# Expert blocks of a token-routed layer: the second product one block later, the middle product in one sum of 512 columns

## The chip, the cores and the metric

The kernel runs on one core of a Trainium2 chip, in one launch. The metric is device time in microseconds (us) from the start of the program to its end.

## What is computed

One layer of a diffusion backbone over 1024 tokens (and 256 context tokens), width 1024. A mixer comes first and is not touched. Then each token goes to two of 16 experts, and the sums are added to the residual stream:

```python
def _moe(xf, w_router, router_bias, w1, w3, w2):
    ...
    padded = (counts + MOE_BLOCK - 1) // MOE_BLOCK * MOE_BLOCK
    ...
    def expert_block(args):
        xblk, e = args
        return (jax.nn.silu(xblk @ w1[e]) * (xblk @ w3[e])) @ w2[e]
```

The 2048 rows (1024 tokens, two experts each) are sorted by expert and cut into blocks of 128 rows (MOE_BLOCK), each of one expert. w1 and w3 are 1024 x 512, w2 is 512 x 1024, all float32. How many blocks an expert has depends on the data; with the inputs timed here there are 23 blocks.

## The kernel before, in words

The program is written engine by engine; every order and every wait is spelled out by hand. The mixer and the router take the first 560 us or so. Then VectorE makes the tables: `slot_tok` (which token is in which slot), `tabs` (a word for each block b: its expert, plus 16 if block b+1 has another expert) and the number of blocks `nb`. Each engine then runs a loop over the blocks, unrolled by two, with branches on `nb` and on the word.

**One product as three.** Every float32 operand is split into a high part, rounded to the fp32r type, and the low rest. `product` (L1536) issues three matmuls for one: high x high, high x low, low x high. For weights, ScalarE copies half a matrix from `raw` to `w1h`, `w3h` or `w2h` (`high`, L729) and VectorE subtracts to make `w1l`, `w3l`, `w2l` (`low`, L1183). For a block's tokens they make `xTh`, `xTl` (`turn_out`), for the hidden rows `hTh` and `hTl` (`hidden_high`, `hidden_low`). There is one set of split weights: the halves of the next expert's w1 can be written only when the last matmul of this expert has read the old half.

**One block on TensorE**, in order (from L1543): 24 matmuls of 512 columns for x @ w1 (bank 2); then x @ w3 in two sums of 256 columns each, q = 0 into bank 3 and q = 1 into bank 4, 24 matmuls each, so that the first half of the hidden rows can be multiplied, transposed and split while the second half is summed; two transposes of the first hidden half stand within the second sum (L1570); then `turn_block(b + 1)`, the eight transposes of the next block's tokens (L1534); then 24 matmuls of 512 columns for hidden @ w2, with the other two transposes (L1590) after the first six.

**The weights' way in.** `raw` has 4 places of one matrix (2 MB) each. SyncE's `load_expert` (L390) issues the 48 loads in the order w1, w3, w2 of expert 0, 1, 2 and so on, each into the place after the one before. A load waits until the matrix that lay in its place, four loads back, is split: w1 of expert e waits for the split of w2 of e-2, w3 of e for w1 of e-1, w2 of e for w3 of e-1.

```python
                    elif not (first and n == 3):
                        sp.wait_ge(w_split[(j + 2) % 3], 2 * e - (2 if j == 0 else 0))
```

In the last block of expert e the two engines split all three matrices of e+1: w1 behind the two halves of x @ w1, w3 behind each sum of 256 columns, w2 behind the two halves of hidden @ w2 (L766 to L790, L1220 to L1235). GpSimd gathers the rows of block b+1 (`gather`, an indirect DMA from `hx_rows` to `xg`), and adds the finished rows into `x_rows` (`add_rows`, L529, an indirect DMA that adds). After the last one comes a short final part that reads `x_rows`, normalises and stores.

Of the kernel before, what the change touches and what calls it, by code (L numbers as in the profile page):

```python
# [26 lines left out]
ALU = mybir.AluOpType  # L27
# [45 lines left out]
def hybrid_block(nc, x, c, ctx_in, c_ctx, w_mod, b_mod, norm1, norm2, w_in, w_gk2, b_gk, w_pool,  # L73
                 pool_scale, gla_gain, w_out, w_router, router_bias, w1, w3, w2, norm_f, inv_counts, out):
    with ExitStack() as stack:
# [68 lines left out]
        with nc.sbuf_tensor("lead_columns", [P, O_G + D], F32), \  # L144
# [73 lines left out]
            tok_ready tok_seen dst_ready dst_seen high_seen split_seen load_seen gathered x_turned xh_ready xT_ready l1a_half l1a l1b l1c silu_done hid_a hid_b hta htb  # L218
            hTh_a hTh_b hT_a hT_b
# [104 lines left out]
        for n, shape in dict(sbias=[NX, NE], hi=[32, 2], lo=[32, 2], t1=[32, 1], t2=[32, 1],  # L324
# [4 lines left out]
                             blkf=[2, NX], posf=[2, NX], prior=[NX, 2 * NGR]).items():  # L329
# [3 lines left out]
        assert rt_at <= ARENA  # L333
        cmp16 = at(O_G + HALF, "p (e k) -> p e k", NE * KC, e=NE)
# [14 lines left out]
        ebf = sb("ebf", [P, NB])  # L349
        new_e = sb("new_e", [P, NB - 1])  # L350

        tabs = sb("tabs", [P, NB + 1], I32)
        T_NB = NB
        NEW = NE

        def entry(eng, b):

            word = eng.value_load(tabs[0:1, bass.ds(b, 1)], min_val=0, max_val=NE + NEW - 1)
            return word & (NE - 1), word

        def place_of(e, j):

            return (e * 3 + j + 3) & (PLACES - 1)

# [4 lines left out]
        def _(sp):  # L369
# [19 lines left out]
            def load_expert(e, turn, first=False):  # L389

                for j, w in enumerate((w1, w3, w2)):
# [3 lines left out]
                    elif first and n == 2:  # L395
                        sp.wait_ge(S["pads_stored"], 16 * 2)
# [31 lines left out]
        def _(pool):  # L428
# [66 lines left out]
            for i in range(2, 9):  # L495
                late_bias(i)
            bc = ("box_chain", [NT])
# [17 lines left out]
            pool.wait_ge(S["pads_stored"], 16 * 2)  # L515
# [8 lines left out]
            def add_rows(b, s):  # L524
# [5 lines left out]
                                        in_=ysb[:, s, :], in_offset=None, compute_op=ALU.add).then_inc(S["y_added"], 16)  # L530
# [4 lines left out]
            nb = pool.value_load(tabs[0:1, T_NB:T_NB + 1], min_val=1, max_val=MAXB)  # L535
            pool.wait_ge(S["x_turned"], 1)
            gather(1)
            pool.wait_ge(S["x2_stored"], 16 * NX)
            pool.sem_inc(S["y_free"], 2)
            pool.wait_ge(S["x_turned"], 2)  # L540
            gather(2)
            pool.wait_ge(S["y_ready"], 4)
            add_rows(0, 0)
            with pool.Fori(0, NB // 2) as pair:
                i = pair * 2
                for s in range(2):
                    with pool.If(i + (s + 1) < nb):
                        b = i + (s + 1)
                        with pool.If(b + 1 < nb):
                            pool.wait_ge(S["x_turned"], b + 2)  # L550
                            gather(b + 2)
                        pool.wait_ge(S["y_ready"], 2 * i + (2 * s + 6))
                        pool.sem_inc(S["dst_seen"], 1)
                        pool.wait_ge(S["y_added"], 16 * b)
                        pool.sem_inc(S["y_free"], 1)
                        add_rows(b, 1 - s)
            pool.wait_ge(S["y_added"], 16 * nb)
            pool.sem_inc(S["moe_done"], 1)
# [9 lines left out]
        def _(act):  # L568
# [121 lines left out]
            for t in range(NX + 2):  # L690
# [20 lines left out]
                if 1 <= t <= NX:  # L711
# [7 lines left out]
                    if w == 0:  # L719
                        for spare in (x_dram, hx_dram):  # L720
                            act.dma_start(spare[PADS:PADS + P, :], x2[:, w, :]).then_inc(S["pads_stored"], 16)
# [7 lines left out]
            def high(j, base, k):  # L729
                act.activation(half_of(j, w_hi[j][:, :], k), half_of(j, raw[:, bass.ds(base, UNIT)], k), ACT.Copy).then_inc(w_high[j], 1)  # L730
# [17 lines left out]
            def hidden_high(b, k):  # L748
                act.wait_ge(S["htb" if k else "hta"], b + 1)
                act.activation(hTh[:, k * 256:(k + 1) * 256], ps[:, 5, k * 256:(k + 1) * 256], ACT.Copy)\  # L750
                    .then_inc(S["hTh_b" if k else "hTh_a"], 1)

            def arrived(j, e):
                act.wait_ge(w_loaded[j], 16 * e + 32)
                act.sem_inc(S["load_seen"], 1)

            act.preload_act_table(ACT.Silu)
            turn_out(0)
            with act.Fori(0, NB // 2) as pair:
                i = pair * 2  # L760
                for s in range(2):
                    with act.If(i + s < nb):
                        b = i + s
                        e, word = entry(act, b)
                        with act.If(word > NE - 1):
                            place = [place_of(e, j) for j in range(3)]  # L766
                            arrived(0, e)
                            act.wait_ge(S["l1a_half"], b + 1)
                            act.sem_inc(S["load_seen"], 1)
                            high(0, place[0] * UNIT, 0)  # L770
                            gate_up(b)
                            high(0, place[0] * UNIT, 1)
                            arrived(1, e)
                            act.wait_ge(S["l1b"], b + 1)
                            act.sem_inc(S["load_seen"], 1)
                            high(1, place[1] * UNIT, 0)
                            hidden_high(b, 0)
                            act.wait_ge(S["l1c"], b + 1)
                            act.sem_inc(S["load_seen"], 1)
                            high(1, place[1] * UNIT, 1)  # L780
                            turn_out(b + 1)
                            hidden_high(b, 1)
                            arrived(2, e)
                            act.wait_ge(S["l2_half"], b + 1)
                            act.sem_inc(S["load_seen"], 1)
                            high(2, place[2] * UNIT, 0)
                            act.wait_ge(S["l2_done"], b + 1)
                            act.sem_inc(S["load_seen"], 1)
                            high(2, place[2] * UNIT, 1)
                        with act.Else():  # L790
                            gate_up(b)
                            hidden_high(b, 0)
                            act.wait_ge(S["l1c"], b + 1)
                            turn_out(b + 1)
                            hidden_high(b, 1)
# [11 lines left out]
        def _(dve):  # L807
# [257 lines left out]
            dve.memset(R["cb"][:, :, 0:8], 0.0)  # L1065
            v(dve.memset(R["cb2"][:, :, 0:8], 0.0))
# [56 lines left out]
            def tables():  # L1123
# [4 lines left out]
                v(dve.tensor_reduce(ebf[:, :], cmpb, AX.X, ALU.add))  # L1128
                v(dve.tensor_scalar(ebf[:, :], ebf[:, :], float(NE - 1), None, ALU.min))
# [487 lines left out]
```

## Time and profile before

| | us |
|---|---|
| median of 3 runs | 1023.66 (1022.66 to 1024.78) |
| the profiled execution, its own time | 1024.93 |
| its span in the trace | 1023.1 |
| expert blocks in it, first matmul to last weighing | 566.89 to 989.30, 422.4 |

The span is the time between the first and the last instruction in the trace; 1.8 us of the execution lie around it. TensorE's rows carry modelled ends, so the length of one matmul is more than it costs in a row of them: the distance from one start to the next is what counts. In the windows view, a line has the stretch, its length, each engine's busy time with its count of instructions, TensorE's granted clock as a share of 2.4 GHz, the DMA engines' busy share, and GB/s.

### The profile page before, as it was taken

The numbers are of one execution on the slowest core, as the hardware profiler recorded it, in microseconds if no ns is written. First come the engines' busy times: TensorE is split into PE (matmuls) and PEld (weight loads), VectorE is DVE, ScalarE is ACT, GpSimd is POOL, SyncE is SP. The second block draws the span as 40 slices with busy tenths as digits, with TensorE's granted clock in tenths as the row PEclk, the third lists the DMA queues.
The fourth block names the chain that finished last, engine by engine and source line by source line (L and its number), as shares of the span: only waits on it lengthen the run. The fifth ranks groups of instructions, "written<-read, shape, count | busy, mean of one in ns | idle before, by whom it ended". The sixth has DMA issues, their size and how long they took to land. (4 is left out here: it accounts for less than half of the span.)

```text
span 1023.1 us, 13258 instructions
## 1 busy us (share of the span) xinstructions
PE 938.6 (92%) x4591; PEld 642.6 (63%) x4592; DVE 598.8 (59%) x804; ACT 355.2 (35%) x476; POOL 190.5 (19%) x212
## 2 busy tenths in 40 slices
PE   4899999999999999999955899999999999999960
PEld 1554544445444445656534788898888988888850
DVE  0246666889433335444438575949967456599933
ACT  1333423100011221212123154637745335477613
POOL 5101000000000010011000132323432233243322
PEclk9699999999999999999975899999999999999985
DMA  9923442420200522111183766979998686699928
GB/s 330 395 82 102 147 165 95 152 82 1 83 0 1 211 116 105 42 42 62 62 300 111 288 206 183 334 241 320 380 362 273 184 305 221 185 339 371 320 40 349
DMA packets 76506, 194.11 MB, mean 190 GB/s; under 512 B 3493, under 2 KB 3626, under 8 KB 76474
## 3 DMA queue, kind: packets, MB, share of 16 engines
q1 hardware_dynamic: 64192, 152.05, 40.9%
q0 software_dynamic: 7680, 25.35, 10.2%
q10 hardware_dynamic: 4602, 16.30, 4.0%
q8 instruction: 19, 0.31, 0.1%
q14 instruction: 13, 0.11, 0.0%
HBM read 167.98 MB, written 25.71 MB: 189 GB/s over the span
## 5 line engine op out<-in xcount | busy, mean ns | idle before, releaser
L1325 PE MATMUL ps<-arena 128*128 128x512 f32 x288 | 128.8, 601 | 0.0
L1333 PE MATMUL ps<-arena 128*128 128x512 f32 (+1 forms) x288 | 119.1, 571 | 0.0
L1464 PE MATMUL ps<-arena 128*128 128x512 f32 x256 | 113.3, 595 | 0.0
L1540 PE MATMUL ps<-w3h,xTh 128*128 128x256 f32 x368 | 105.9, 288 | 0.0
L1540 PE MATMUL ps<-w3h,xTl 128*128 128x256 f32 x368 | 104.1, 283 | 0.0
L1540 PE MATMUL ps<-w3l,xTh 128*128 128x256 f32 x368 | 104.1, 283 | 0.0
L1333 PEld LDWEIGHTS ps<-arena 128*128 128x128 f32 x288 | 54.0, 190 | 64.3 <-issue 62.7
L1325 PEld LDWEIGHTS ps<-arena 128*128 128x128 f32 x288 | 54.2, 193 | 62.5 <-issue 62.5
L1187 DVE TENSOR_TENSOR w1l<-raw,w1h 128x2048 fp32r<-128x2048 f32 x30 | 68.6, 2287 | 29.8 <-ACT w1h L730 29.7
L1464 PEld LDWEIGHTS ps<-arena 128*128 128x128 f32 x256 | 47.4, 190 | 54.4 <-issue 53.6
L730 ACT ACTIVATE w1h<-raw 128x2048 fp32r (+1 forms) x32 | 61.1, 1912 | 58.0 <-PE ps L1540 46.2
L1540 PE MATMUL ps<-w2h,hTh 128*128 128x512 f32 x184 | 76.9, 418 | 0.8 <-DVE hTl L1200 0.4
L1540 PE MATMUL ps<-w1h,xTh 128*128 128x512 f32 x184 | 72.7, 395 | 3.2 <-DVE xTl L1180 3.2
L1540 PE MATMUL ps<-w1h,xTl 128*128 128x512 f32 x184 | 72.3, 393 | 0.0
L1540 PE MATMUL ps<-w1l,xTh 128*128 128x512 f32 x184 | 72.3, 393 | 0.0
L1540 PE MATMUL ps<-w2h,hTl 128*128 128x512 f32 x184 | 72.2, 393 | 0.0
L1540 PE MATMUL ps<-w2l,hTh 128*128 128x512 f32 x184 | 72.2, 393 | 0.0
L1187 DVE TENSOR_TENSOR w2l<-raw,w2h 128x2048 fp32r<-128x2048 f32 x32 | 71.8, 2285 | 0.0
L1540 PEld LDWEIGHTS ps<-w3l,xTh 128*128 128x128 f32 x368 | 70.5, 192 | 0.9
L730 ACT ACTIVATE w2h<-raw 128x2048 fp32r (+1 forms) x32 | 61.1, 1917 | 28.9 <-PE ps L1540 22.9
L1540 PEld LDWEIGHTS ps<-w3h,xTh 128*128 128x128 f32 x368 | 70.4, 191 | 0.9
L1187 DVE TENSOR_TENSOR w3l<-raw,w3h 128x2048 fp32r<-128x2048 f32 x31 | 70.9, 2286 | 0.0
(244 smaller groups left out, 1496.5 us busy)
## 6 DMA issues: line engine op xcount, KB each, us to landing
raw<-in_w_dram SPq DMA_DIRECT2D x48, 2048.0 KB, 12.9
arena<-in_w_mod_dram SPq DMA_DIRECT2D x12, 2048.0 KB, 8.0
arena<-in_w_in_dram SPq DMA_DIRECT2D x4, 2048.0 KB, 15.2
x_rows<-arena ACTq DMA_DIRECT2D x9, 512.0 KB, 2.6
hx_rows<-arena ACTq DMA_DIRECT2D x9, 512.0 KB, 2.6
arena<-in_x_dram SPq DMA_DIRECT2D x8, 512.0 KB, 14.5
arena<-in_w_out_dram SPq DMA_DIRECT2D x2, 2048.0 KB, 9.3
arena<-in_x_dram ACTq DMA_DIRECT2D x8, 512.0 KB, 10.5
```

The costliest lines, as they stand in the source:

```text
L730: act.activation(half_of(j, w_hi[j][:, :], k), half_of(j, raw[:, bass.ds(base, UNIT)], k), ACT.Copy).then_inc(w_high[j], 1)
L1187: dve.tensor_tensor(half_of(j, w_lo[j][:, :], k), half_of(j, raw[:, bass.ds(base, UNIT)], k), half_of(j, w_hi[j][:, :], k).bitcast(F32), A ...
L1325: ins = pe.matmul(ps[:, bank, :], hxT[:, k, g[1] * P:(g[1] + 1) * P], w[:, k, :], start=(k == 0), stop=(k == KC - 1))
L1333: ins = pe.matmul(ps[:, bank, 0:m * P], w[:, k, col:col + P], hxT[:, k, t0 * P:(t0 + m) * P], start=(k == 0), stop=(k == KC - 1))
L1464: ins = pe.matmul(ps[:, 5 + h, :], m, w[:, k, :], start=(k == 0), stop=(k == KC - 1))
L1540: ins = pe.matmul(out_ap, parts[l][:, lhs], w_parts[w][:, cols], start=start and n == 0, stop=stop and n == 2)
```

## The change

Four things change, all in the expert blocks.

1. **The second layer comes one block later.** TensorE's body for block b (`pe_block`) is x @ w1 of block b (`gate_part`), four transposes of the hidden rows of block b-1 (`turn_hidden`), x @ w3 of block b (`up_part`), the eight transposes of the tokens of block b+1, and then hidden @ w2 of block b-1 (`out_of_hidden`). Block 0 has a first part of its own in front of the loop, and the last block's hidden @ w2 follows the loop.
2. **x @ w3 is one sum of 512 columns** in bank 3; `hidden`, `hidden_high` and `hidden_low` each work on 512 columns at once, after all of it.
3. **w2 is split at that point.** w2 of expert e was split in the last block of e-1; it is now split in the first block of e (`own_down`), behind the two halves of hidden @ w2 of the block before. The word in `tabs` gets 32 more if block b-1 had another expert. w1 and w3 of the next expert are still split in the last block of this one (`next_gate`, `next_up`).
4. Around it: gathers run one block further ahead; the last block's rows go out from `xg`; the spare rows of `hx_rows` are filled by GpSimd from `ident`, not by ScalarE's queue; the table needs one more small VectorE instruction. `load_expert` is untouched but for the count of `pads_stored`.

```diff
-        def half_of(j, unit, k):
-
-            if j == 1:
-                return unit.rearrange("p (k n) -> p k n", k=KC)[:, :, k * 256:(k + 1) * 256]
+        def half_of(unit, k):
...
@@ ScalarE
+            def next_gate(b, e, k):
+
+                if k == 0:
+                    after(w_loaded[0], 16 * e + 32)
+                after(S["l1a" if k else "l1a_half"], b + 1)
+                high(0, place_of(e, 0) * UNIT, k)
...
+            def own_down(b, e, k):
+
+                if k == 0:
+                    after(w_loaded[2], 16 * e + 16)
+                after(S["l2_done" if k else "l2_half"], b)
+                high(2, place_of(e - 1, 2) * UNIT, k)
...
+            def act_block(b, par):
+                e, word = entry(act, b)
+                with act.If((word & LAST) > 0):
+                    next_gate(b, e, 0)
+                    act.wait_ge(S["hid_done"], b)
+                    gate_up(b)
+                    hidden_high(b - 1)
+                    next_gate(b, e, 1)
+                    next_up(b, e, 0)
+                    turn_out(b + 1)
+                    next_up(b, e, 1)
...
+                with act.If(word > FIRST - 1):
+                    own_down(b, e, 0)
+                    own_down(b, e, 1)
@@ VectorE
+            def dve_block(b, par):
+                e, word = entry(dve, b)
+                with dve.If((word & LAST) > 0):
+                    low(0, place_of(e, 0) * UNIT, e + 1, 0)
+                    hidden_low(b - 1)
+                    low(0, place_of(e, 0) * UNIT, e + 1, 1)
+                    hidden(b)
+                    low(1, place_of(e, 1) * UNIT, e + 1, 0)
+                    turn_out(b + 1)
+                    low(1, place_of(e, 1) * UNIT, e + 1, 1)
...
+                weigh(b - 1, ysb[:, 1 - par, :])
+                with dve.If(word > FIRST - 1):
+                    low(2, place_of(e - 1, 2) * UNIT, e, 0)
+                    low(2, place_of(e - 1, 2) * UNIT, e, 1)
...
+            hidden_low(nb - 1)
+            weigh(nb - 1, xg)
@@ TensorE
-                        for q, done in enumerate(("l1b", "l1c")):
...
-                                ins = product(ps[:, 3 + q, 0:256], x_parts, slice(k * P, (k + 1) * P), (w3h, w3l),
-                                              slice(col, col + 256), k == 0, k == KC - 1)
...
+            turn_x(0)
+            gate_part(0, 0)
+            up_part(0)
+            turn_x(1)
+
+            def pe_block(b, par):
+                e, word = entry(pe, b)
+                pe.wait_ge(S["silu_done"], b)
+                gate_part(b, e)
+                turn_hidden(b - 1)
+                up_part(e)
+                turn_x(b + 1)
+                pe.wait_ge(S["y_ready"], 2 * b)
+                out_of_hidden(b - 1, (e + (word >> 5) * (NE - 1)) & (NE - 1))
+
+            blocks(pe, nb, pe_block)
+            turn_hidden(nb - 1)
+            pe.wait_ge(S["y_ready"], 2 * nb)
+            out_of_hidden(nb - 1, NE - 1)
```

ScalarE's instructions in the last block of an expert, from the first half of w1, before (ISA and REGISTER_ALU are waits and addresses; `arena` at L746 is the silu, at L754 in the changed kernel):

```order
L730 ACTIVATE w1h<-raw 128x2048
L746 ACTIVATE arena<-ps 128x512 [waits l1a]
L730 ISA
L730 ACTIVATE w1h<-raw 128x2048
L730 REGISTER_ALU [waits w_loaded_w3,l1b]
L730 REGISTER_ALU
L730 ISA
L730 ACTIVATE w3h<-raw 128x8x256
L750 ACTIVATE hTh<-ps 128x256 [waits hta]
L730 ISA [waits l1c]
L730 ACTIVATE w3h<-raw 128x8x256
```

and in the changed kernel:

```order
L738 ACTIVATE w1h<-raw 128x2048
L754 ACTIVATE arena<-ps 128x512 [waits l1a,hid_done]
L758 ACTIVATE hTh<-ps 128x512 [waits ht_done]
L738 ISA [waits l1a]
L738 ACTIVATE w1h<-raw 128x2048
L738 REGISTER_ALU [waits w_loaded_w3,l1b_half]
L738 REGISTER_ALU
L738 ISA
L738 ACTIVATE w3h<-raw 128x2048
L749 REGISTER_ALU
L750 ACTIVATE xTh<-ps 128x1024 [waits x_turned]
```

The copy of the hidden rows (`hTh`) stood behind w3's first half, on the block's own rows; it now stands straight behind w1's first half and the silu, on the rows of the block before. It is the copy for which hidden @ w2 of that block waits.

VectorE at the end of that block, before:

```order
L1187 ISA [waits w_high_w3]
L1187 TENSOR_TENSOR w3l<-raw,w3h 128x8x256
L1208 REGISTER_ALU [waits y_free,l2_done]
L1208 SCALAR_TENSOR_TENSOR arena<-ps,slot_w,arena 128x512 x2
L1187 REGISTER_ALU [waits w_high_w2]
L1187 REGISTER_ALU
L1187 ISA
L1187 TENSOR_TENSOR w2l<-raw,w2h 128x2048
L1187 ISA [waits w_high_w2]
L1187 TENSOR_TENSOR w2l<-raw,w2h 128x2048
```

and in the changed kernel, at the end of the first block of an expert (`arena` at L1208 and L1234 is the weighing):

```order
L1234 ISA [waits l2_done,y_free]
L1234 SCALAR_TENSOR_TENSOR arena<-ps,slot_w,arena 128x512 x2
L1269 COMPARE_AND_BRANCH
L1214 REGISTER_ALU
L1214 ISA
L1216 ISA [waits w_high_w2]
L1216 REGISTER_ALU
L1216 ISA
L1216 TENSOR_TENSOR w2l<-raw,w2h 128x2048
L1214 REGISTER_ALU
L1216 ISA [waits w_high_w2]
L1216 TENSOR_TENSOR w2l<-raw,w2h 128x2048
```

The two subtractions of w2 still stand last, behind the weighing; what moved is the block in which they stand, from the last one of the expert before to the first one of w2's own expert.

## Rows read from the trace of the kernel before

**Rows 1.** The page, part 1: busy time, share and instructions of each engine.

```profile
PE 938.6 (92%) x4591; PEld 642.6 (63%) x4592; DVE 598.8 (59%) x804; ACT 355.2 (35%) x476; POOL 190.5 (19%) x212
```

**Rows 2.** The `raw` tile alone, by block: us, DVE busy, ACT busy, clock, DMA.

```profile
660.08:678.09 18.01, 4.83 (x3) 1.92 (x1) 1.00 1.05 376
...
696.39:714.71 18.32, 13.56 (x7) 11.50 (x6) 1.00 0.98 309
...
951.54:971.01 19.47, 13.72 (x7) 11.29 (x7) 1.00 0.92 324
...
sum 422.41, DVE 210.35 ACT 172.29; mean DVE 9.15 ACT 7.49
```

**Rows 3.** Timeline of TensorE, first and last matmuls of w1 and w3: start, length.

```profile
587.12 0.39 PE L1540 MATMUL ps<-w1h,xTh 128*128 128x512 f32 x1
...
592.33 0.39 PE L1540 MATMUL ps<-w1h,xTl 128*128 128x512 f32 x1
592.56 0.28 PE L1540 MATMUL ps<-w3h,xTh 128*128 128x256 f32 x1
...
596.75 0.28 PE L1540 MATMUL ps<-w3h,xTl 128*128 128x256 f32 x1
```

**Rows 4.** Chain of waits, 650 to 656 us: eight transposes.

```profile
653.33 0.87 PE ps L1534 x8
```

**Rows 5.** Timeline of all engines, 860 to 867 us: start, length, engine, line.

```profile
860.29 0.39 PE L1540 MATMUL ps<-w1h,xTh 128*128 128x512 f32 x1
...
860.59 1.41 DVE L1208 SCALAR_TENSOR_TENSOR arena<-ps,slot_w,arena 128x512 f32<-128x512 f32 x2
...
861.92 4.48 DVE L1187 TENSOR_TENSOR w2l<-raw,w2h 128x2048 fp32r<-128x2048 f32 x2
...
865.06 2.82 POOL L529 DMA_INDIRECT x_rows<-arena,block_dst  x1 [0.82 <-POOL block_dst L526]
```

**Rows 6.** Timeline of SyncE's queue: the load behind that conversion.

```profile
866.73 0.37 SPq L405 DMA_DIRECT2D raw<-in_w_dram  x1
```

**Rows 7.** DMA issues at 853.3 us and at 866.7 us: size, us to landing.

```profile
raw<-in_w_dram SPq DMA_DIRECT2D x1, 2048.0 KB, 8.4
...
raw<-in_w_dram SPq DMA_DIRECT2D x1, 2048.0 KB, 12.5
```

**Rows 8.** Timeline of ScalarE, 955 to 972 us: conversions behind late loads.

```profile
956.99 1.92 ACT L730 ACTIVATE w1h<-raw 128x2048 fp32r x1 [3.05 <-DMA raw<-in_w_dram]
958.81 0.58 ACT L746 ACTIVATE arena<-ps 128x512 f32<-128x512 f32 x1
...
969.77 3.72 ACT L730 ACTIVATE w2h<-raw 128x2048 fp32r x2 [2.26 <-DMA raw<-in_w_dram]
```

**Rows 9.** Chain of waits, 944 to 967 us, behind a late load.

```profile
944.62 17.30 DMA raw<-in_w_dram
...
962.33 1.68 ACT w3h L730
...
964.15 0.38 ACT hTh L750
...
964.55 0.43 DVE hTl L1200
...
965.22 1.62 PE ps L1540 x6
```

**Rows 10.** Timeline of the first block: VectorE, TensorE.

```profile
565.44 1.23 DVE L1180 TENSOR_TENSOR xTl<-ps,xTh 128x1024 fp32r<-128x1024 f32 x1 [0.95 <-ACT xTh L742]
...
566.89 0.79 PE L1540 MATMUL ps<-w1h,xTh 128*128 128x512 f32 x1 [3.25 <-DVE xTl L1180]
...
574.55 0.28 PE L1540 MATMUL ps<-w3h,xTh 128*128 128x256 f32 x1
```

**Rows 11.** All engines by stretch, counts in brackets, then TensorE's clock.

```profile
566.89:571.30 4.41, 4.41 (x10) 3.47 (x11) 4.41 (x3) 0.00 (x0) 0.00 (x0) 0.50 1.02 391
571.40:575.00 3.60, 3.60 (x19) 3.01 (x18) 1.86 (x1) 0.25 (x1) 0.00 (x0) 1.00 1.02 419
```

More of the change, by code:

```diff
@@ L363, in place_of, with blocks @@
             return (e * 3 + j + 3) & (PLACES - 1)
+        def blocks(eng, nb, body):
+            with eng.Fori(0, NB // 2 - 1) as pair:
+                i = pair * 2
+                for s in range(2):
+                    with eng.If(i + (s + 1) < nb):
+                        body(i + (s + 1), 1 - s)
         block = stack.enter_context(nc.Block())
@@ L534, in _, with pool_block @@
             pool.wait_ge(S["table_ready"], 1)
[L535 to L537 removed]
+            nb = pool.value_load(tabs[0:1, T_NB:T_NB + 1], min_val=NE, max_val=MAXB)
             pool.wait_ge(S["x2_stored"], 16 * NX)
             pool.sem_inc(S["y_free"], 2)
[L540 to L541 removed]
+            for g in range(1, 4):
+                pool.wait_ge(S["x_turned"], g)
+                gather(g)
             pool.wait_ge(S["y_ready"], 4)
[L543 to L556, printed above, removed]
+            add_rows(0, ysb[:, 0, :])
+            def pool_block(b, par):
+                with pool.If(b + 2 < nb):
+                    pool.wait_ge(S["x_turned"], b + 3)
+                    gather(b + 3)
+                pool.wait_ge(S["y_ready"], 2 * b + 4)
+                pool.sem_inc(S["dst_seen"], 1)
+                pool.wait_ge(S["y_added"], 16 * b + 16)
+                pool.sem_inc(S["y_free"], 1)
+                add_rows(b, ysb[:, par, :])
+            blocks(pool, nb - 1, pool_block)
+            pool.wait_ge(S["y_ready"], 2 * nb + 2)
+            pool.sem_inc(S["dst_seen"], 1)
             pool.wait_ge(S["y_added"], 16 * nb)
+            pool.sem_inc(S["dst_seen"], 1)
+            add_rows(nb - 1, xg)
+            pool.wait_ge(S["y_added"], 16 * nb + 16)
             pool.sem_inc(S["moe_done"], 1)
@@ L757, in _ @@
+            def own_down(b, e, k):
+                if k == 0:
+                    after(w_loaded[2], 16 * e + 16)
+                after(S["l2_done" if k else "l2_half"], b)
+                high(2, place_of(e - 1, 2) * UNIT, k)
             act.preload_act_table(ACT.Silu)
             turn_out(0)
[L759 to L795, printed above, removed]
@@ L797, in _ @@
+            blocks(act, nb, act_block)
+            hidden_high(nb - 1)
             act.wait_ge(S["moe_done"], 1)
@@ L1529, in _, with turn_x @@
             pe.sem_inc(S["y_ready"], 2)
-            def turn_block(b):
+            x_parts, h_parts = (xTh, xTl), (hTh, hTl)
+            def turn_x(b):
                 pe.wait_ge(S["gathered"], 16 * b + 16)
@@ new lines, in into_hidden @@
+            def into_hidden(bank, w_parts, split, e, half, done):
+                for k in range(KC):
+                    if k % 4 == 0:
+                        pe.wait_ge(split, 2 * e + (k // 4 + 1))
+                    ins = product(ps[:, bank, :], x_parts, slice(k * P, (k + 1) * P), w_parts,
+                                  slice(k * HALF, (k + 1) * HALF), k == 0, k == KC - 1)
+                    if k == 3:
+                        ins.then_inc(S[half], 1)
+                ins.then_inc(S[done], 1)
@@ new lines, in gate_part, with up_part, turn_hidden @@
+            def gate_part(b, e):
+                pe.wait_ge(S["xT_ready"], b + 1)
+                into_hidden(2, (w1h, w1l), w_split[0], e, "l1a_half", "l1a")
+            def up_part(e):
+                into_hidden(3, (w3h, w3l), w_split[1], e, "l1b_half", "l1b")
+            def turn_hidden(b):
+                pe.wait_ge(S["hid_done"], b + 1)
+                for m in range(4):
+                    ins = pe.transpose(ps[:, 4, m * P:(m + 1) * P], hid[:, m * P:(m + 1) * P], ident[:, :])
+                ins.then_inc(S["ht_done"], 1)
@@ new lines, in out_of_hidden @@
+            def out_of_hidden(b, e):
+                pe.wait_ge(S["hT_ready"], b + 1)
+                for k in range(4):
+                    if k % 2 == 0:
+                        pe.wait_ge(w_split[2], 2 * e + (k // 2 + 1))
+                    for h in range(2):
+                        col = k * D + h * HALF
+                        ins = product(ps[:, 5 + h, :], h_parts, slice(k * P, (k + 1) * P), (w2h, w2l),
+                                      slice(col, col + HALF), k == 0, k == 3)
+                    if k == 1:
+                        ins.then_inc(S["l2_half"], 1)
+                ins.then_inc(S["l2_done"], 1)
```

191 lines of the change are left out of this document (76 added, 115 removed).

## The prediction

> **What bounds the kernel now.** The page comes first: TensorE is busy for 938.6 us of the span, 92%, and no other engine is over 59% [rows 1]. The change touches only the expert blocks, so I read the windows of that stage next, for the tile `raw` alone: 23 blocks in 422.41 us. Where ScalarE copies nothing of a new expert (x1 is a leftover of the block before) a block takes 18.01 us, where it copies all three matrices of the next one (x6) 18.3 us, and one block near the end takes 19.47 us [rows 2]. Fifteen blocks convert the next expert's w1: 1, 3, 4, 6 to 9, 11, 13, 15 and 17 to 21, counted from 0. So experts 0, 1, 3, 7, 8, 9 and 10 have two blocks, the others one.
>
> Then the price of one matmul, from start to start in TensorE's timeline. The 24 of w1 start from 587.12 to 592.33 us, 0.2265 us apart; 36 of w3, with 256 columns, from 592.56 to 596.75, 0.1197 us apart [rows 3]. Eight transposes take 0.87 us, 0.109 each [rows 4]. A block of before is 48 x 0.2265 + 48 x 0.1197 + 12 x 0.109 = 17.93 us. It measures 18.01: TensorE sets the pace with no gap, and a block with a new expert loses some 0.3 us more.
>
> The loads are the second thing to read. Three loads and a block's gather and store nearly fill the DMA engines where experts have one block each (share 0.98 in such a block [rows 2]). In the block of 19.47 us the chain of waits already goes through a load: 17.30 us from issue to landing, then ScalarE's w3 copy, hTh, hTl, and only then TensorE [rows 9]. ScalarE and VectorE work strictly in the order written, so what waits for a landing holds back the hidden rows behind it.
>
> **The change, part by part.**
>
> *TensorE's work per block* becomes 72 x 0.2265 + 12 x 0.109 = 17.62 us [rows 3, 4]: 0.39 less than 18.01, 0.68 less than 18.3. One sum of 512 columns gives 24 x (2 x 0.1197 - 0.2265) = 0.31 of it; the rest is the small waits for hTl that go.
>
> By the Trainium skill (TensorE: Matmul & The Clock Gate, section Back-to-back issue gap) N columns cost N/2.4 + 2.5 ns, so two of 256 cost 218.4 ns and one of 512 costs 215.8: the gain would be 0.06 us a block in place of 0.31. The rows differ (239.4 against 226.5), and the measurement decides.
>
> *The ring of loads* loses a block of slack, and this decides my forecast. w1 of expert k goes into the place of w2 of k-2. Before, that w2 was split in the last block of k-3; now it is split at the end of the first block of k-2. How long after that end can be read, since the same instructions stand at the same place: the next block starts at 860.29, VectorE weighs from 860.59 for 1.41 us, subtracts w2 from 861.92 for 4.48 us [rows 5], and SyncE issues the load at 866.73 [rows 6]. That is 6.4 us into the next block. But if experts k-2 and k-1 have one block each, that next block is the one in which w1 of k must be copied. This holds for k = 6, 7, 13, 14 and 15: blocks 8, 9, 19, 20, 21.
>
> Such a block, from its start at 0: issue at 6.4. A load alone lands after 8.4 us; one beside the adding store after 12.5 [rows 7]. The store is issued 4.8 us into the block (865.06 [rows 5]), so it runs beside the load; I take 9.4, near the lower end, since the queue is otherwise empty: w1 lands at 15.8. Then ScalarE starts 0.4 us after the landing (961.92, 962.33 [rows 9]) and copies for 1.92 [rows 8], VectorE subtracts for 2.24 [rows 5] after some 0.5 of handing over, hTl of 512 columns (0.43 for 256 [rows 9], 0.6 estimated) follows with 0.2 to TensorE: hidden @ w2 can start 5.9 us after the landing. In an undisturbed block it starts at 12.2 us. Any landing after 6.3 us therefore stops TensorE, and this one can't be before 14.8.
>
> w3 of k is issued right behind w1 and lands after it: conversions of w1, w3 and w2 started at 956.99, 962.33 and 969.77 where the loads were queued [rows 8, 9], so 5.3 to 7.4 us apart; I take 6.4, the middle. Behind w3's landing stand the copy (0.4 + 1.92), the subtraction (0.5 + 2.24) and only then xTl (1.23 [rows 10], some 0.1 to TensorE): the next block starts 6.4 us after that landing. A stopped block so takes 6.4 + 9.4 + 6.4 + 6.4 = 28.6 us; 26.5 with the lower ends of both loads, 32.7 with the upper ones. Five are 143.0 (132.5 to 163.5).
>
> *The opening.* w1 of block 0 takes 7.66 us (566.89 to 574.55 [rows 10]), partly at half clock, as before; w3 5.44; transposes 0.87. Then nothing covers the way of block 1's tokens through xTh and xTl, since hidden @ w2 of block 0 stands a block later: 3.25 us, the wait that the first block shows now [rows 10]. The sum is 17.2. In that pause the clock may fall: ten matmuls at 0.50 took 4.41 us where nineteen at 1.00 took 3.60 [rows 11], 2 us in all. I take 1.0.
>
> *The closing.* Block 22 is the first of expert 15: a body of 17.6, then its own hidden @ w2, whose hTl stands behind weighing (0.3 + 1.4) and w2's two subtractions (4.48 [rows 5]) on VectorE. With hTl and handover that is a pause of 6.9 us, then 5.44 of matmuls, 0.3 to the weighing, and 2.0 for a fallen clock [rows 11]: 32.3.
>
> *Nothing for the rest.* VectorE's 13.56 us for `raw` in such a block [rows 2] and under 4 us for the other steps fit into 17.6. The earlier gathers, the spare rows from GpSimd and the ScalarE issue saved lie beside TensorE's mixer work. If the first gather then waited for them it would cost its own time, but it starts long after. The table's extra VectorE step is on the path, 0.3 us (hTl of 256 columns takes 0.43 [rows 9]). The adding stores shift with the blocks; the last one stays exposed as before.
>
> **The sum.** 17.2 + 1.0 + 16 x 17.62 + 143.0 + 32.3 = 475.4 against 422.4: 53.0 more, with the table 53.3. From the profiled execution's 1024.93 that is 1078.2; the median lies 1.3 below that execution, so **1077**. Own range 1063 to 1098: the stopped blocks move it by -10.5 and +20.5, the clock by -3.
>
> **The rivals.**
>
> *The loads stay covered; faster.* Had w1 of k landed within 6.3 us of the block's start, all 21 bodies would take 17.62: 370.0, an opening of 17.2, and a closing of 17.6 + 1.8 (copy and subtraction of the hidden rows) + 5.44 + 0.3 = 25.2. That is 412.4, 10.0 less than 422.4, so 1014. For it: the ring now hides loads that take up to 17.30 us [rows 9] at a cost of one block of 19.47 [rows 2]. Against it: their issue was early, and now the issue alone is at 6.4. Chance 0.08.
>
> *The DMA engines alone set the pace of single-block experts.* The ring holds, but five blocks cost 19.5 us as block 21 does now [rows 2]: 9.4 more than that, 1024. For it: the share of 0.98. Against: DMA is idle while the ring waits. Chance 0.06, split evenly over the three signs.
>
> *The sum of 512 columns is not what it says.* Gain 0.06 in place of 0.31 a block: 23 x 0.25 = 5.8 more, 1083. Against: w1's matmuls have exactly that form and their row is plain [rows 3]. Chance 0.05.
>
> *The pauses cost the clock too.* Nine us of waiting stand ahead of hidden @ w2 in each stopped block. At 0.50 the 24 matmuls take 5 us longer by [rows 11], of which about 1.5 hides behind w3's way. Five times 3.5: 1095. Against: in rows 11 the clock was back after ten matmuls. Chance 0.12.
>
> The Trainium skill (the same page, Part 1: The HAM clock gate) has the lower clock as the default that activity releases, which speaks for this one; rows 11 show both levels, 1.2 and 2.4 GHz.
>
> **How the numbers follow.** The forecast has 0.69. Faster: 0.08 + 0.02 = 0.10. Within 0.2% (2 us, about what a measurement of this kernel can tell): 0.02. Slower: 0.88. The range 1060 to 1098 takes in the forecast with nearly all of its bounds, the dearer sum and most of the clock case, and leaves out the two cheap ones.
>
> **What would show it.** Ordinary bodies at 17.6 us; blocks 8, 9, 19, 20, 21 at 26 to 33, each with ScalarE's w1 copy released by a load that was issued some 6 us into that block; a pause ahead of hidden @ w2; a pause of 3 us after block 0 and of 7 ahead of the last product. It is wrong if those loads are issued before their block starts, or if TensorE runs on past them.

## The result, and the profile after

The changed kernel takes **1100.97 us** (median of 4 runs, 1099.51 to 1102.84) against 1024.22 beside it: 1.0752 times as long, 95% interval 1.073 to 1.0775. The forecast was 1077 with a range to 1098. So the direction was right, and the size too small by 24 us. The profiled execution took 1100.29 us, 75.4 more than the one of before.

Page of the changed kernel, part 1, the granted clock of part 2, and three groups of part 5:

```profile
PE 935.4 (85%) x4039; PEld 620.8 (57%) x4040; DVE 592.8 (54%) x760; ACT 351.3 (32%) x453; POOL 186.2 (17%) x213
...
PEclk8899999999999999999569999977999999788885
...
L1575 PE MATMUL ps<-w2h,hTh 128*128 128x512 f32 x184 | 78.9, 429 | 71.0 <-DVE hTl L1226 71.0
...
L1216 DVE TENSOR_TENSOR w1l<-raw,w1h 128x2048 fp32r<-128x2048 f32 x30 | 68.6, 2286 | 97.3 <-ACT w1h L738 97.3
...
L738 ACT ACTIVATE w1h<-raw 128x2048 fp32r (+1 forms) x32 | 61.2, 1915 | 116.2 <-DMA raw<-in_w_dram 86.9
```

Read the right-hand column from the bottom up. ScalarE waited 86.9 us for the landing of w1, VectorE 97.3 for ScalarE's copy of it, TensorE 71.0 for hTl behind that. TensorE's busy time for the whole program is hardly less than before (935.4 against 938.6 [rows 1]). In the expert blocks it is 3.5 us more, 424.26 in the first row below against 420.80 in this window of before:

```profile
566.89:989.30 422.41, 420.80 (x2484) 369.11 (x2484) 299.38 (x252) 220.32 (x182) 131.54 (x88) 0.99 0.82 272
```

So there the fallen clock (0.92 against 0.99) takes more than the shorter products give.

Windows of the changed kernel: the whole stage, then blocks 0, 8, 9, 10, 19, 20, 21, and block 22 with the closing product. The columns are us, PE, PEld, DVE, ACT, POOL busy, granted clock, DMA share, GB/s.

```profile
565.82:1064.26 498.44, 424.26 (x1932) 349.75 (x1932) 293.39 (x206) 216.43 (x159) 125.80 (x88) 0.92 0.69 231
...
565.82:582.13 16.31, 13.77 (x56) 11.12 (x57) 8.46 (x5) 1.62 (x2) 1.15 (x2) 0.89 0.94 359
...
707.72:739.96 32.24, 20.03 (x86) 16.25 (x84) 16.44 (x12) 13.03 (x9) 5.74 (x4) 0.79 0.68 237
739.96:774.23 34.27, 19.95 (x86) 16.21 (x85) 17.88 (x12) 13.14 (x9) 5.85 (x4) 0.80 0.62 214
774.23:791.92 17.69, 17.69 (x86) 14.74 (x84) 8.66 (x8) 5.95 (x5) 5.74 (x4) 1.00 0.55 163
933.47:965.34 31.87, 19.93 (x86) 16.21 (x84) 16.01 (x12) 13.03 (x9) 5.85 (x4) 0.79 0.70 244
965.34:999.56 34.22, 19.90 (x86) 16.16 (x84) 17.92 (x12) 13.15 (x9) 5.74 (x4) 0.80 0.63 215
999.56:1030.98 31.42, 19.33 (x86) 15.65 (x84) 15.54 (x12) 12.64 (x9) 5.85 (x4) 0.84 0.67 234
1030.98:1064.00 33.02, 26.35 (x113) 21.09 (x112) 16.62 (x13) 8.82 (x8) 9.18 (x4) 0.90 0.21 32
```

The first window ends 0.2 us ahead of the last weighing (1064.45 us). Counted to the weighing, as for the kernel before, the stage takes 498.6 us in place of 422.4 [rows 2]. Fifteen blocks (2 to 7, 10 to 18) take 17.69 each, and exactly the five named ahead are stopped: 164.0 us together. Inside one of them, ScalarE's timeline, block 8 (start 707.72):

```profile
726.61 1.91 ACT L738 ACTIVATE w1h<-raw 128x2048 fp32r x1 [16.61 <-DMA raw<-in_w_dram]
728.42 0.58 ACT L754 ACTIVATE arena<-ps 128x512 f32<-128x512 f32 x1
728.90 0.59 ACT L758 ACTIVATE hTh<-ps 128x512 fp32r<-128x512 f32 x1
...
733.23 1.91 ACT L738 ACTIVATE w3h<-raw 128x2048 fp32r x1 [1.94 <-DMA raw<-in_w_dram]
735.04 1.01 ACT L750 ACTIVATE xTh<-ps 128x1024 fp32r<-128x1024 f32 x1
```

GpSimd's and SyncE's queues at that place, and DMA issues, loads of w1 alone, at 714.4 and 747.2 us (size, us to landing):

```profile
712.69 2.81 POOL L535 DMA_INDIRECT x_rows<-arena,block_dst  x1 [0.83 <-POOL block_dst L532]
```

```profile
714.38 2.28 SPq L408 DMA_DIRECT2D raw<-in_w_dram  x3
```

```profile
raw<-in_w_dram SPq DMA_DIRECT2D x1, 2048.0 KB, 11.8
...
raw<-in_w_dram SPq DMA_DIRECT2D x1, 2048.0 KB, 13.3
```

The load is issued 6.7 us into the block (forecast 6.4), 1.7 us behind the adding store, and lands after 11.8 us, not 9.4. The hidden rows' copy stands behind w1's on ScalarE, so TensorE waits for 12.2 us, up to 732.3. In block 9 the chain of waits does not go through w3 at all:

```profile
747.18 13.30 DMA raw<-in_w_dram
760.95 1.92 ACT w1h L738
...
765.47 0.70 DVE hTl L1226
...
766.67 8.39 PE ps L1575 x27
```

It goes from w1's landing to hidden @ w2 and from there straight to the next block. That product runs on a fallen clock; windows of block 8 show both levels, 1.2 GHz and then 2.4:

```profile
732.30:736.60 4.30, 4.27 (x10) 3.41 (x11) 3.38 (x3) 3.38 (x3) 0.00 (x0) 0.50 1.00 399
736.80:739.90 3.10, 3.10 (x15) 2.56 (x14) 3.10 (x3) 2.86 (x2) 0.00 (x0) 1.00 0.04 15
```

### The profile page after: what moved, and what is told of

The parts are those of the page before. It is cut to its first block, busy times and chain, and to the rows that moved or that the text cites. A ratio compares the mean times of both kernels' runs of the same rounds, so it can differ in the third digit from the quotient of the medians.

```text
span 1098.5 us, 12326 instructions
## 1 busy us (share of the span) xinstructions
PE 935.4 (85%) x4039; PEld 620.8 (57%) x4040; DVE 592.8 (54%) x760; ACT 351.3 (32%) x453; POOL 186.2 (17%) x213
## 4 chain that ended last, share of the span: by engine, by line
PE 73%; DMA 10%; DVE 8%; issue 4%; ACT 2%; DVEq 1%; ACTq 1%; SPq 1%; POOL 0%; POOLq 0%
PE ps L1575 28%; PE ps L1366 11%; PE ps L1358 10%; PE ps L1497 10%; DMA raw<-in_w_dram 7%; DMA arena<-in_w_mod_dram 2%; PE ps L1569 1%; DVE w2l L1216 1%; PE ps L1514 1%; DMA arena<-x_rows 1%; PE ps L1296 1%; PE ps L1471 1%; PE ps L1475 1%; PE ps L1377 1%; PE ps L1430 1%
## 5 line engine op out<-in xcount | busy, mean ns | idle before, releaser
L1216 DVE TENSOR_TENSOR w1l<-raw,w1h 128x2048 fp32r<-128x2048 f32 x30 | 68.6, 2286 | 97.3 <-ACT w1h L738 97.3
L738 ACT ACTIVATE w1h<-raw 128x2048 fp32r (+1 forms) x32 | 61.2, 1915 | 116.2 <-DMA raw<-in_w_dram 86.9
L1575 PEld LDWEIGHTS ps<-w2h,hTh 128*128 128x128 f32 x184 | 37.6, 204 | 79.9 <-issue 72.4
L1575 PE MATMUL ps<-w2l,hTh 128*128 128x512 f32 x184 | 76.0, 413 | 0.0
L1575 PE MATMUL ps<-w2h,hTl 128*128 128x512 f32 x184 | 75.8, 412 | 0.0
L1575 PE MATMUL ps<-w3h,xTh 128*128 128x512 f32 x184 | 73.6, 400 | 0.0
L1575 PE MATMUL ps<-w3h,xTl 128*128 128x512 f32 x184 | 71.9, 391 | 0.0
L1575 PE MATMUL ps<-w3l,xTh 128*128 128x512 f32 x184 | 71.8, 390 | 0.0
L738 ACT ACTIVATE w3h<-raw 128x2048 fp32r (+1 forms) x32 | 61.1, 1912 | 13.3 <-DMA raw<-in_w_dram 8.5
```

What stands on the lines that cost most here:

```text
L738: act.activation(half_of(w_hi[j][:, :], k), half_of(raw[:, bass.ds(base, UNIT)], k), ACT.Copy).then_inc(w_high[j], 1)
L1216: dve.tensor_tensor(half_of(w_lo[j][:, :], k), half_of(raw[:, bass.ds(base, UNIT)], k), half_of(w_hi[j][:, :], k).bitcast(F32), ALU.subtra ...
L1575: ins = pe.matmul(out_ap, parts[l][:, lhs], w_parts[w][:, cols], start=start and n == 0, stop=stop and n == 2)
```

## The experiments

Theory: the whole loss is the ring of loads, whose w1 of expert k waits for w2 of k-2. Rivals: an order in the queues that makes the stop, a landing that is late by itself, the clock. late_before, small_store, queue_order, down_first, clock and clock12 were timed once each; the kernels that were timed more often spread over 2.4 to 4.4 us.

**ring.** The changed kernel with the loads in another order: w1 and w3 of e+1 go ahead of w2 of e, so that w1 of k takes the place of w2 of k-3 again, which is split a block sooner. w2 of expert 0 is split in block 0.

```diff
+            def turn_of(e, turn):
+                load(0, e + 1, 3 * turn + 2, 2, 2 * e - 2)
+                load(1, e + 1, 3 * turn + 3, 0, 2 * e + 2)
+                load(2, e, 3 * turn + 4, 1, 2 * e + 2)
...
-            return (e * 3 + j + 3) & (PLACES - 1)
+            return (e * 3 + (2 if j == 0 else 3)) & (PLACES - 1)
```

> The changed kernel with the loads issued in another order: w1 and w3 of expert e+1, then w2 of expert e. w1 of k then waits for the split of w2 of k-3, not k-2. Theory (the ring of four places, w2 held a block longer): blocks 8, 9, 19, 20 and 21, 164.0 us together after the change, go back to 17.7 us each, plus up to 8 us where the DMA engines fall behind: 1026 to 1034 us. Rival (the DMA engines alone set the pace of single-block experts): these five stay at 19.6 us or more, 1036 or above. Rival (the pipelined order itself is the loss): near 1101.

Measured: 1026.67 us, ratio 1.0022 (1.001 to 1.0035). No block is stopped: 2 to 21 take 17.69 each but for 17.92 and 17.84 (blocks 11 and 12). Windows of this kernel, the stage and block 22 with the closing product, both up to the end of the last product:

```profile
565.62:988.07 422.45, 413.16 (x1932) 342.41 (x1932) 293.61 (x206) 220.63 (x161) 135.11 (x88) 0.98 0.81 272
...
955.25:988.07 32.82, 26.15 (x113) 20.93 (x112) 16.66 (x13) 10.26 (x8) 9.69 (x4) 0.90 0.43 113
```

Counted to the last weighing (988.51 us) the stage is back at 422.9 us, against 422.4 before, so the loss of 75 us lies in the order of the loads. Nothing is won either: blocks 2 to 21 are 11.3 us shorter than before, and the ends give it back. Blocks 0, 1 and 22 with the closing take 15.93 + 19.46 + 32.82 = 68.2, against 20.23 + 18.33 + 18.00 = 56.6.

**late_before.** The kernel before, with w1 of e waiting for w2 of e-1 in place of e-2. That w2 is split at the end of the block ahead of the one in which w1 must be copied, if e-1 has one block: the changed kernel's dependence without its other parts.

```diff
-                        sp.wait_ge(w_split[(j + 2) % 3], 2 * e - (2 if j == 0 else 0))
+                        sp.wait_ge(w_split[(j + 2) % 3], 2 * e)
```

> The kernel before with one wait moved: w1 of expert e waits for the split of w2 of e-1 in place of e-2. Nothing else. Theory (the ring): every block that is the only one of its expert (4, 7, 8, 9, 18 to 21) stops for its load and takes some 35 us: 1130 to 1165 us. Rival (the loss comes from the new order of the products, not from the ring): below 1045.

Measured: 1149.17 us. Blocks 4, 7, 8, 9 and 18 to 21 take 33.6 to 35.0 us, all others 18.0 or 18.3 (block 0: 20.2). The chain of waits in block 7 (start 710.73) and ScalarE's copy behind the landing:

```profile
717.14 11.89 DMA raw<-in_w_dram
```

```profile
729.52 1.91 ACT L730 ACTIVATE w1h<-raw 128x2048 fp32r x1 [16.50 <-DMA raw<-in_w_dram]
```
 A load whose place comes free only with the block before (it is issued 6.4 us into this one) makes the same stop in a kernel whose second layer isn't moved. It does so eight times, since here one expert with a single block is enough, where the changed kernel needs two in a row.

**small_store.** The changed kernel with the adding store of a block's rows replaced by a store of 16 columns; the output so lacks the experts' part.

```diff
-                pool.indirect_dma_start(out=x_dram, out_offset=bass.IndirectOffsetOnAxis(ap=block_dst[:, :], axis=0),
-                                        in_=y, in_offset=None, compute_op=ALU.add).then_inc(S["y_added"], 16)
+                pool.dma_start(x_dram[PADS:PADS + P, 0:16], y[:, 0:16]).then_inc(S["y_added"], 16)
```

> The changed kernel without the adding store: a small store of 16 columns takes its place, so the output lacks the experts' part. Theory (the store beside the load makes the landing late: 11.5 to 13.2 us where 9.4 was forecast): w1 of the stopped blocks lands 8.4 to 9 us after its issue, each stopped block takes some 29 us, and the last store's 6 us go to 2: 1078 to 1088 us. Rival (a load after a pause lands late whatever lies beside it): landings stay at 11.5 or more, 1093 to 1097.

Measured: 1078.67 us. DMA issues of w1 at 714.8 and 744.3 us, then the windows of blocks 8 and 9:

```profile
raw<-in_w_dram SPq DMA_DIRECT2D x1, 2048.0 KB, 8.4
...
raw<-in_w_dram SPq DMA_DIRECT2D x1, 2048.0 KB, 8.6
```

```profile
708.21:737.10 28.89, 20.11 (x85) 16.31 (x84) 16.18 (x12) 13.06 (x9) 3.47 (x4) 0.82 0.67 250
737.10:767.26 30.16, 20.61 (x85) 16.69 (x84) 17.54 (x12) 13.15 (x9) 3.58 (x4) 0.83 0.61 226
```

The two loads behind w1 are still there, the gather too, and w1 lands in 8.4 to 8.6: the 3.2 to 4.8 us more in the changed kernel come from the adding store. Whether its adding or its 512 KB make them, this run can't tell, since it takes away both. The five blocks take 146.6 us in place of 164.0; another 4.5 of the 22.3 us saved is the last store, which nothing hides and which lands in 1.7 us, not 6.2.

**queue_order.** The changed kernel with the silu and hTh ahead of both of w1's copies on ScalarE, xTh ahead of w3's, and VectorE's steps alike.

```diff
-                    next_gate(b, e, 0)
                     act.wait_ge(S["hid_done"], b)
                     gate_up(b)
                     hidden_high(b - 1)
+                    next_gate(b, e, 0)
                     next_gate(b, e, 1)
-                    next_up(b, e, 0)
                     turn_out(b + 1)
+                    next_up(b, e, 0)
                     next_up(b, e, 1)
```

> The changed kernel with the late loads kept, but silu and hTh ahead of w1's copies, xTh ahead of w3's, and VectorE alike. Theory (the strict order behind a landing makes the stop long): hidden @ w2 runs at once, the next block starts when w1's first half is split, some 26 to 28 us after the start in place of 31.4 to 34.3: 1062 to 1080 us. Rival (the ring's wait alone counts, the order behind it doesn't): 1095 to 1101.

Measured: 1101.92 us, on the rival's side and a miss of mine. Hidden @ w2 of block 8 runs at once (12.2 to 17.5 us into it), but the next load hardly comes sooner: w1's loads of blocks 8 and 9 are issued 32.4 us apart (718.03 and 750.42), where the changed kernel has 32.8. The five blocks do take 158.6 us in place of 164.0, but block 10 (19.44) and the last one with the closing (3.0 more) give that back. This made me form a second theory: a stop is one turn of a **loop**. Landing of w1; six subtractions, the weighing and the rest on VectorE up to w2's split; issue of the next w1; its landing. Whatever TensorE gets sooner is lost unless this turn is shorter.

**down_first.** queue_order with w2's copies and subtractions ahead of w3's in blocks that are first and last of their expert.

```diff
@@ ScalarE
                     turn_out(b + 1)
-                    next_up(b, e, 0)
-                    next_up(b, e, 1)
...
                     own_down(b, e, 1)
+                with act.If((word & LAST) > 0):
+                    next_up(b, e, 0)
+                    next_up(b, e, 1)
```

> queue_order with one more move: in a block that is first and last of its expert, w2's copies and subtractions stand ahead of w3's on ScalarE and VectorE. The loop theory: a stop is one turn of a loop through the queues, landing of w1, VectorE's subtractions and weighing in their order up to w2's split, the next load's issue, its landing; so w2's split and the issue come some 4.5 us (w3's two subtractions) earlier: 32.5 us from issue to issue become 28, with w1's landing still 11.6 to 13.2 after its issue, and blocks 4, 7 and 18, where w3 now comes later, become 2 to 4 us longer each; total 1085 to 1092 against queue_order's 1101.9. Rival: the landing of w3, or the store and the gather beside it, sets the pace, not VectorE's order: issue to issue stays 32 to 33 us and the total is 1100 to 1110.

Measured: 1080.62 us, less than the 1085 to 1092 that I expected. SyncE's queue, and the windows of blocks 8, 9, 19, 20, 21:

```profile
717.95 0.38 SPq L408 DMA_DIRECT2D raw<-in_w_dram  x1
...
744.68 1.00 SPq L408 DMA_DIRECT2D raw<-in_w_dram  x2
```

```profile
711.35:738.88 27.53, 19.77 (x86) 15.72 (x84) 17.27 (x12) 15.27 (x11) 5.74 (x4) 0.91 0.74 249
738.88:765.47 26.59, 20.55 (x85) 16.49 (x85) 16.95 (x12) 12.91 (x10) 5.85 (x4) 0.89 0.78 274
928.07:955.66 27.59, 18.16 (x86) 14.58 (x84) 17.27 (x12) 15.26 (x11) 5.85 (x4) 0.94 0.74 252
955.66:982.35 26.69, 19.86 (x84) 15.92 (x85) 16.94 (x12) 12.91 (x10) 5.74 (x4) 0.88 0.80 271
982.35:1009.32 26.97, 20.02 (x85) 16.15 (x85) 16.96 (x12) 12.91 (x10) 5.85 (x4) 0.88 0.82 278
```

Issue to issue is now 26.7 to 26.9 us. Between blocks 8 and 9 the turn is 5.7 us shorter than in queue_order: w3's two subtractions account for some 4.5, and w1's landing for 1.3 (11.7 after its issue, 13.0 there). That is the loop theory's mark: what is taken out of the turn comes off it. The delay of w3 that I put on blocks 4, 7 and 18 shows in the blocks behind them (block 5: 20.43 us, 2.7 more; blocks 8 and 19 some 1 us longer than 9 and 20) and is smaller in sum.

**clock, clock12.** The changed kernel with 24 or 12 products of no use in front of hidden @ w2, in blocks that are first and last of their expert.

```diff
+                with pe.If(word > FIRST + LAST - 1):
+                    pe.wait_ge(S["g2_loaded"], 16)
+                    for n in range(24):
+                        pe.matmul(ps[:, 7, :], ident[:, :], g2b[:, 0:HALF], start=True, stop=True)
```

> The changed kernel with 24 products of no use (128x512, float32, into a spare bank) in front of x@w2's second layer in every block that is first and last of its expert, so that TensorE works while it would wait. Their cost: in the three such blocks that are not stopped (4, 7, 18) all of it is added, some 10.6 us each, 30 us in all; in the stopped blocks most of it lies in the stop. If the clock's loss is what makes x@w2 take 7.4 us there in place of 5.3, the stopped blocks' x@w2 now takes 5.3 to 5.6, and each of these blocks is 0.8 to 2 us shorter than in the changed kernel: total 1123 to 1129. If the 7.4 us have another cause (a wait for w2's halves inside it), it stays 7 us and more, and the stopped blocks keep their length: total 1130 to 1134.

Measured: 1190.49 us, a miss, and no test of the question. Such a product costs 0.858 us, not the 0.44 I had reckoned: all eight blocks take 38.29 us, 24 x 0.858 more than 17.69, and no stop is left in which the clock could fall. So half of them:

> As clock, with 12 products in place of 24. In clock one such product took 0.858 us (20.6 us for 24), twice what was reckoned, so that TensorE was never idle there at all; 12 take 10.3 us and lie in the stop of some 12 us, so x@w2 starts when it is allowed to (24.3 to 26.7 into the block) but at a higher clock. If the clock is what the 7.4 us come from, the five stopped blocks take 30.0 to 32.0 us in place of 31.4 to 34.3 (1.5 to 2.1 less each, about 9 in all) and the blocks 4, 7 and 18 take 28.0: total 1100.97 + 30.9 - 9 = 1121 to 1125. If the clock has no part in it, the stopped blocks keep 31.4 to 34.3: total 1131 to 1133.

Measured: 1131.28 us, again in the rival's range. Windows of blocks 19 and 20, and TensorE's timeline in block 19, where the clock never fell:

```profile
964.71:996.11 31.40, 28.43 (x109) 19.03 (x108) 15.15 (x11) 12.56 (x9) 5.85 (x4) 1.00 0.67 234
996.11:1030.41 34.30, 30.00 (x108) 20.49 (x109) 18.27 (x12) 13.50 (x10) 5.75 (x4) 0.95 0.62 214
```

```profile
989.22 0.49 PE L1575 MATMUL ps<-w2h,hTh 128*128 128x512 f32 x1 [1.80 <-DVE hTl L1226]
996.11 0.49 PE L1575 MATMUL ps<-w1h,xTh 128*128 128x512 f32 x1 [1.18 <-DVE xTl L1209]
```

At full clock hidden @ w2 of block 19 takes 5.3 us from its first start to its last, not 7.3, and yet the block is only 0.46 us shorter (31.41), little more than blocks 8 and 19 of the changed kernel differ by (0.37): TensorE then waits 1.18 us for xTl. Block 21, at full clock too, is shorter by 0.1. So in these two blocks the clock's loss is mostly hidden behind w3's way. In block 20 the useless products ended 4.3 us too soon, the clock fell again, and the length stayed; that block is no test.

**ring_two.** ring with x @ w3 as two sums of 256 columns each (banks 3 and 7).

```diff
+                    for q in range(1 if bank == 2 else 2):
+                        n = HALF if bank == 2 else 256
+                        ins = product(ps[:, bank + 4 * q, 0:n], x_parts, slice(k * P, (k + 1) * P), w_parts,
+                                      slice(k * HALF + q * n, k * HALF + (q + 1) * n), k == 0, k == KC - 1)
```

> ring with x@w3 as two sums of 256 columns each again (banks 3 and 7), nothing else moved. By the rows of the kernel before (48 products of 256 columns take 5.75 us where 24 of 512 take 5.44) it costs 0.31 us in each of 23 blocks, 7.1 us in all: 1033 to 1034.5. Rival, that the 256-column form costs as much as two halves of 512 plus 0.06 us a block: 1027.5 to 1028.5. If the products' form were worth nothing: 1026 to 1027.

Measured: 1031.87 us, ratio 1.0081 (1.0065 to 1.0096), some 6 us over ring and 1.1 under the range that I expected. Window of block 4:

```profile
637.30:655.29 17.99, 17.99 (x110) 16.02 (x108) 12.89 (x11) 11.47 (x8) 4.87 (x4) 1.00 0.99 328
```

Every ordinary block takes 17.99 in place of 17.69: 0.30 us, where the rows said 0.31. The Trainium skill's formula for the gap of an isolated matmul (TensorE: Matmul & The Clock Gate, section Back-to-back issue gap) gives an estimate of 0.06; the trace does not agree, and this run decides for the rows.

**ring_best.** ring with the last block written out by hand.

```diff
+            up_part(NE - 1)
+            pe.wait_ge(S["y_ready"], 2 * m + 2)
+            out_of_hidden(m, (NE - 1 + (word >> 5) * (NE - 1)) & (NE - 1), True)
...
+            act.wait_ge(S["l2_done"], m + 1)
+            hidden_high(m + 1)
+            with act.If(word > FIRST - 1):
+                own_down(m + 1, NE - 1, 1)
```

> The loads in the new order as in ring, and the last block written out by hand. The transposes of its hidden rows stand in the middle of the second layer of the block before; ScalarE makes hTh right after that layer, ahead of the second half of w2's copy; VectorE takes w2's first half ahead of the weighing; the eight transposes for a block that is not there are gone. In ring the pause between the last two second layers is 973.0 to 980.4, 7.4 us, and the layer behind it runs its first 4.4 us at half the clock (1.9 us lost). By the waits of ring VectorE then needs 972.7 to 977.0 for w2's first half (2.2), hTl (0.7) and the weighing (1.4), so the pause is about 4.0 us; with the transposes' 0.9 and less of the clock's loss the kernel saves 4 to 6 us on ring's 1026.7: 1020.5 to 1023, ratio 0.9965 to 0.999 to the kernel before, so just faster than both. Rival: another wait ends the pause (w2's copy or the adding store ahead of the last weighing), and under 2 us are saved: 1025 to 1027.

Measured: 1024.73 us, ratio 1.0008 (0.9999 to 1.0017): level with before, short of what I expected. Its last block with the closing takes 28.0 us in place of 32.8, as reckoned, but the block starts late, and a block with late loads (11) took 19.77:

```profile
962.24 0.47 PE L1613 MATMUL ps<-w1h,xTh 128*128 128x512 f32 x1 [2.58 <-issue]
```

"issue" says that the profile shows nothing that was waited for. I put it down to the loop's empty turns, the tests for blocks that are not there; the next run puts that to the test.

**ring_best_six.** ring_best with these turns in groups.

```diff
-            with eng.Fori(0, NB // 2 - 1) as pair:
-                i = pair * 2
+            with eng.Fori(0, 5) as six:
+                with eng.If(six * 6 + 1 < nb):
+                    with eng.Fori(0, 3) as pair:
+                        i = six * 6 + pair * 2
```

> ring_best with the loop over the blocks written as five groups of six blocks, each group behind one test of its own. In ring_best the last block began 2.6 us late with nothing waited for (TensorE's row says issue): the loop's empty turns for the blocks 22 to 30 now stand ahead of the last block, where in ring they lay behind the last first layer's work, in the pause. With one group passed over at one test and two blocks' tests left of the other, some 2 us of the 2.6 should go; each group's start may add 0.1 to 0.3 us (four starts): 1022.5 to 1024.5, ratio 0.9985 to 1.0002. Rival: the late start has another cause (the load of the last word), and nothing is gained: 1024.5 to 1025.5.

Measured: **1022.03 us** (11 runs, 1020.78 to 1023.34), ratio 0.9984 (0.9974 to 0.9994): 0.16% faster than the kernel before, and 0.5 us under the range that I expected. The same row, the stage, and the start of the closing product:

```profile
957.07 0.47 PE L1615 MATMUL ps<-w1h,xTh 128*128 128x512 f32 x1 [0.28 <-issue]
```

```profile
566.02:985.09 419.07, 412.36 (x1924) 341.27 (x1924) 292.48 (x205) 219.45 (x160) 132.07 (x88) 0.99 0.81 273
```

```profile
977.89 0.50 PE L1615 MATMUL ps<-w2h,hTh 128*128 128x512 f32 x1 [3.25 <-DVE arena L1264]
```

The idle time went from 2.58 to 0.28 us, with four failing tests in place of nine, and the wait ahead of the closing product is 3.25 us, where ring had 6.1.

## Why the prediction was right or wrong

The sum, term by term (measured against forecast, us):

| term | forecast | measured |
|---|---|---|
| opening, block 0 | 17.2 | 16.3 |
| block 1, with the clock's 1.0 | 18.6 | 19.4 |
| 15 ordinary blocks | 264.3 | 265.4 |
| five stopped blocks | 143.0 | 164.0 |
| closing, to the weighing | 32.3 | 33.5 |
| sum | 475.4 | 498.6 |

*Right.* The step that decided it (w1 of k takes the place of w2 of k-2, whose split comes a block later) is shown from both sides: taken out by ring, put alone into the old kernel by late_before. The five blocks, the way of the wait through ScalarE's w1 copy and hTl, and the price of 512 columns (ring_two) came as written. The pauses of the opening and closing stand where they were put, each 0.7 us shorter (2.55 and 6.17).

*Wrong: the size of a stopped block,* 28.6 forecast and 32.8 measured on average. Its four pieces, five blocks added:

| piece | forecast | measured |
|---|---|---|
| start to issue of w1 | 32.0 | 34.3 |
| issue to landing of w1 | 47.0 | 61.6 |
| landing of w1 to landing of w3 | 32.0 | 30.6 |
| landing of w3 to next start | 32.0 | 37.5 |

The step that failed is "I take 9.4, near the lower end, since the queue is otherwise empty". I had two rows, 8.4 alone and 12.5 beside the adding store [rows 7], and had just written that the store runs beside this load. In block 8 the store is issued 1.7 us ahead of it and ends 1.7 us before it lands. The right row was the upper one; with 12.3 in place of 9.4 the five blocks give 157.5 and the forecast 1091.5. small_store shows it: without the adding store 8.4 to 8.6 us, and five blocks of 146.6 us together. The upper bounds of the forecast, 32.7 a block, do come to 163.5, but that is luck: they had 7.4 us between the landings of w1 and w3, where 6.1 were measured on average, and the clock, which they left out, and a later issue (6.9 us into the block in place of 6.4) filled the gap.

What the last piece has too much I put down to the clock, which the forecast had at 0 and a rival at 3.5 us in every block. By the chain of block 9 it costs some 2 us where w1's way ends last (blocks 9, 20): xTl was ready 1.9 us ahead of the next block in both. Where w3's way does it costs less: xTl of block 8 was ready 1.0 us ahead of the next block, and clock12 had blocks 19 and 21 shorter by 0.46 and 0.1. That is an estimate of some 5.5 in all, neither the forecast's 0 nor the rival's 17.5. For blocks 9 and 20, its larger part, it is read from the trace alone; no run kept the clock up there.

*The rival of 1014 was reckoned wrong.* ring is exactly its case, and it gave 1026.67. Its closing of 25.2 us left out that w2 of the last expert is still split between the last two products: 33.3 measured, to the weighing. Its clock after block 0's pause was left out too (1.8). Had I added these, the gain would have been nil before any run, and this rival would have stood at no change.

Not tried: a fifth place in `raw`, and a second buffer for w2's parts. Whether the late loads of block 11 (17.92, 19.77 and 18.75 us in three kernels with the same order of loads) are chance or a matter of timing stays open.

## What to carry to other kernels

When a step is moved later, list what it frees, and count for each load that waits for that place how many blocks are left between its issue and its use; experts with one block are the case that decides. When such a wait can't be covered, price it as a turn of a loop (landing, the in-order work up to the release, issue), with the load's time taken beside the traffic that will run with it, not alone. And a pipeline that is skewed by one stage pays at both ends; here that took all that 20 shorter blocks had earned, until the last block was written out by hand and the empty turns ahead of it were grouped.

## What the runs showed of the hardware

- A 2 MB load takes 8.4 us alone [rows 7], 8.4 to 8.6 with plain loads queued behind it (small_store), and 11.6 to 13.3 beside a GpSimd store that adds 128 rows of 4 KB in DRAM (changed kernel).
- A float32 product of 512 columns that isn't split into two parts costs 0.858 us at full clock (run clock), nearly four times the 0.2265 of one of the split ones.
- TensorE's clock stood at 0.50 for the first 4.3 us of work after a stop of 12 us (block 8 of the changed kernel). With useless products in most of the stop (clock12) it stayed at 1.00 in blocks 19 and 21, after idle gaps of 1.80 and 1.99 us, and fell for 3.4 us in 8, 9 and 20, after gaps of 1.93, 4.38 and 4.29.
- With nine failing tests of a loop ahead of its next product TensorE stood idle for 2.58 us (ring_best), with four for 0.28 (ring_best_six). In ring, where such turns lie beside the pause ahead of the closing product, VectorE's hTl came 0.45 us of "issue" late.
